# Two re-orderings on VectorE in a hybrid decoder trunk: weight-sum splits before a block's products, and S5 matrix steps spread over two groups

## The reference, cut to what matters

```
h = x + 1/2 * SwiGLU_a(RMSNorm(x))                    # w_ffn1_gu, w_ffn1_down
u = RMSNorm(h); P = u @ W_in                          # GLA heads and S5 heads
h = h + concat(GLA out, S5 out) @ W_out
h = h + CrossAttn(RMSNorm(h), memory K/V)
h = h + 1/2 * SwiGLU_b(RMSNorm(h))                    # w_ffn2_gu, w_ffn2_down
y = RMSNorm_final(h)
swiglu(x) = (silu(g) * u) @ w_down, with g, u = split(x @ w_gu)
S5: ab = exp(dt*L); bb = (ab - 1)/L * b; x_t = ab * x_{t-1} + bb u_t; y = Re(C x) + D u
```

## Time and profile before

| | |
|---|---|
| median of 3 runs | 1297.46 us (1296.92 to 1297.63) |
| the profiled execution | 1296.79 us, of which its span is 1295.0 us |
| TensorE (PE) busy | 1270.0 us, 98% of the span, 10275 matmul records |
| PE weight loads busy | 1230.6 us, 95% |
| VectorE busy | 861.3 us, 67% |
| ScalarE busy | 527.3 us, 41% |
| GpSimd busy | 350.0 us, 27% |

### The profile page before, as it was taken

One profiled execution on the slowest core, in us unless ns is written; L12 is line 12 of the kernel. 1 busy time (PEld: TensorE's weight loads), 2 busy tenths in 40 slices (PEclk: granted clock), 3 DMA queues, 4 the chain that ended last, 5 costly groups with the idle time before them and its releaser, 6 DMA issues.

```text
span 1295.0 us, 24300 instructions
## 1 busy us (share of the span) xinstructions
PE 1270.0 (98%) x10275; PEld 1230.6 (95%) x10275; DVE 861.3 (67%) x1056; ACT 527.3 (41%) x797; POOL 350.0 (27%) x409
## 2 busy tenths in 40 slices
PE   7999999999999999999999999999999999999997
PEld 6999999999999999999999997599999999999997
DVE  4987379844789736558565537478895589637952
ACT  6544145521223422565443224246453255414543
POOL 0025623276896202000002100032230133102321
PEclk9999999999999999999999999999999999999998
DMA  6232233263213442125423656322233323223221
GB/s 185 81 89 82 82 98 98 82 131 88 83 55 85 90 91 63 53 66 153 120 83 97 203 204 225 133 82 79 84 96 85 98 82 99 83 83 96 86 62 73
DMA packets 227148, 129.95 MB, mean 100 GB/s; under 512 B 22240, under 2 KB 221392, under 8 KB 227024
## 3 DMA queue, kind: packets, MB, share of 16 engines
q1 hardware_dynamic: 223168, 123.37, 33.4%
q10 hardware_dynamic: 3872, 5.04, 1.1%
HBM read 121.42 MB, written 5.78 MB: 98 GB/s over the span
## 4 chain that ended last, share of the span: by engine, by line
PE 89%; DVE 6%; ACT 2%; issue 2%; DMA 0%; SPq 0%; DVEq 0%; ACTq 0%
PE PS L723 86%; PE PS L1315 1%; DVE wl L1967 1%; DVE xl L2076 1%; DMA AR<-in_x_prompt 0%; PE PS L791 0%; ACT wh L1453 0%; DVE PS L2055 0%; ACT gua L1599 0%; DVE PS L2221 0%; DVE Hs L2376 0%; PE PS L1401 0%; DVE gua L2151 0%; PE PS L1293 0%; PE PS L933 0%
## 5 line engine op out<-in xcount | busy, mean ns | idle before, releaser
L1453 ACT ACTIVATE wh<-raw 128x1024 fp32r<-128x1024 f32 (+1 forms) x128 | 132.2, 1033 | 377.0 <-PE PS L723 376.9
L723 PE MATMUL PS<-yh,wh 128*128 128x288 f32 x960 | 206.1, 296 | 2.5 <-DVE yl L2164 1.6
L723 PE MATMUL PS<-yl,wh 128*128 128x288 f32 x960 | 205.0, 295 | 0.0
L723 PE MATMUL PS<-yh,wl 128*128 128x288 f32 x960 | 205.0, 295 | 0.0
L1967 DVE TENSOR_TENSOR wl<-raw,wh 128x1024 fp32r<-128x1024 f32 (+1 forms) x128 | 160.1, 1251 | 62.6 <-ACT wh L1453 61.3
L723 PE MATMUL PS<-xh,wh 128*128 128x288 f32 x768 | 171.7, 305 | 0.3 <-DVEq L2146 0.2
L723 PE MATMUL PS<-xh,ARr 128*128 128x288 f32 x768 | 169.5, 296 | 0.3
L723 PE MATMUL PS<-xh,wl 128*128 128x288 f32 x768 | 164.9, 297 | 0.0
L723 PE MATMUL PS<-xl,wh 128*128 128x288 f32 x768 | 164.8, 296 | 0.0
L723 PEld LDWEIGHTS PS<-yh,wh 128*128 128x128 f32 x960 | 154.0, 188 | 4.2 <-DVE yl L2164 1.8
L723 PEld LDWEIGHTS PS<-yh,wl 128*128 128x128 f32 x960 | 154.3, 188 | 0.0
(11 more groups left out here) (370 smaller groups left out, 2217.0 us busy)
## 6 DMA issues: line engine op xcount, KB each, us to landing
raw<-in_w_ffn_gu SPq DMA_DIRECT2D x88, 512.0 KB, 3.9
raw<-in_w_ffn_down SPq DMA_DIRECT2D x32, 512.0 KB, 4.0
raw<-in_w_in SPq DMA_DIRECT2D x16, 512.0 KB, 4.1
raw<-in_w_ckv SPq DMA_DIRECT2D x16, 512.0 KB, 3.9
raw<-in_w_ffn_down SPq DMA_DIRECT2D x16, 384.0 KB, 3.4
Hs<-in_cache_mem_k SPq DMA_DIRECT2D x6, 1024.0 KB, 7.0
raw<-in_w_out SPq DMA_DIRECT2D x8, 512.0 KB, 4.0
raw<-in_w_cq SPq DMA_DIRECT2D x8, 512.0 KB, 5.1
```

The costliest lines, as they stand in the source:

```text
L723: return e.matmul(out, lhsT, rhs, start=start, stop=stop, **kw)
L1453: e.activation(wh[:, n % 2, 0:K * P], raw[:, n % 4, 0:K * P], ACT.Copy).then_inc(w_hi, 1)
```

## The change

Three places of VectorE's code are edited; no instruction is added or taken away, and the streams of all other engines stay as they are.

```diff
             def third_group(i, n, par):
 
                 plain_low(i, n, par, groups[4])
-                matrix_step(3 * i + par)
-                if par:
-                    matrix_step(3 * i + 2)
+                first = 2 * i + par + (max(0, i - 2) if not par else max(0, i - 1))
+                matrix_step(first)
+                if not par and i >= 2:
+                    matrix_step(first + 1)
 
             def third_down(i, n, par):
 
                 normed(groups[5])(i, n, par)
-                if 2 * i + par < 6:
-                    matrix_step(18 + 2 * i + par)
+                matrix_step(16 + 2 * i + par)
...
             for n in range(8):
+                if n == 7:
+                    low_sums(0)
                 e.wait_ge(mm_done, seq(n) + 3)
                 hidden(n // 2, n, n % 2, groups[0])
...
-                elif n == 7:
-                    low_sums(0)
                 plain_low(n // 2, n, n % 2, groups[0])
...
+                if b == 3:
+                    low_sums(FIRST_FFN2)
                 e.wait_ge(mm_done, seq(n) + 3)
                 hidden(i, n, b % 2, g)
                 if b:
                     conv(n + 2)
-                if b == 3:
-                    low_sums(FIRST_FFN2)
                 plain_low(i, n, b % 2, g)
```

## The result

The changed kernel took 1302.31 us (median of 6 runs, 1300.59 to 1304.42) against 1297.55 us of the kernel before on the same chip (6 runs, 1296.87 to 1299.55). The ratio is 1.0037, with an interval of 1.0024 to 1.0049: slower by some 4.8 us. The forecast was 1300.9, in a range of 1297.6 to 1303.0. The profiled execution took 1301.25 us, its span 1299.4 against 1295.0.

A forecast was written before the change was run, and what follows sets the result against it. TensorE, 89% of the last-ending chain, was the bound, so only its waits count. -1.3 - 1.0 + 4.5 - 0.5 + 1.7 = +3.4 us on 1296.79 gave 1300.2; median forecast 1300.9, range 1297.6 to 1303.0.

The forecast's parts named there:

- Edit 1: At two first units, low_sums goes ahead of the block's wait: -0.65 us each, -1.3 us for two.
- The gap before S1: TensorE's stop after product A11 at a first unit, 1.71 us idle, 1.88 us lost; was to go.
- the one before S3: TensorE's wait ahead of product seven at a first unit, to grow from 0.57 to some 1.8 us.
- The rival of full gain: Product seven is ready when TensorE comes, so each first unit gives 1.88 us, 3.76 in all; chance 0.11.
- Edit 2: Group 3's matrix steps: yl unchanged (0), one step behind it instead of two, -1.0 us at the third down block.
- the gap: TensorE's wait at 401.47 before the third down block, 0.84 us idle plus 0.17; was to go whole, -1.0 us.
- one L2219 takes 1.3 to 2.5 us: Single step behind yl, where a pair took 3.8 us; conv was to start by 397.8 and end by 400.1.
- Edit 3: Last two matrix steps: step 23 behind the last down block's work, so TensorE starts the transposes 4.5 us late.
- The refill: In s5_matrices, transpose rounds no longer wait for ScalarE: 7.4 us becomes 6.8 to 6.9, -0.5 us.
- The clock: After the stop before the transposes, clock at 0.50 for some 3.4 us of work: +1.7 us, between 0 and +3.4.

The follow-up runs named there:

- e5: Kernel before with both low_sums ahead of the block's wait, and the last plain block's L2164 put behind the next unit's four sums; 1290.74 us, ratio 0.9955.
- e1: Kernel before with only both low_sums moved ahead of the block's wait; 1295.63 us, ratio 0.9986.
- e3: Changed kernel with the down group's matrix steps given out earlier, none after its last two blocks; 1295.16 us, ratio 0.9992 to the kernel before.
- e4: Changed kernel with 34 unread matmuls ahead of TensorE's wait for the last matrix step; 1302.38 us, ratio 1.0046 to the kernel before.
- e6: Changed kernel with the down group's matrix steps given out earlier, none after its last block; 1296.43 us, ratio 0.9999 to the kernel before.
- e9: Changed kernel with 30 unread matmuls ahead of TensorE's wait for the last matrix step; 1303.44 us, ratio 1.0045 to the kernel before.
- e10: Changed kernel run again without an edit; 1301.57 us, ratio 1.0035 to the kernel before.
- e2: Changed kernel with both low_sums put back, so only the matrix steps are moved; 1303.44 us, ratio 1.0052 to the kernel before.
- e8: e5 with yl ahead of conv as in e7, 15 steps in group 3, nine over down blocks 0 to 6; 1292.27 us, ratio 0.9965.
- e7: Kernel before with group 3's last yl (L2164) ahead of the conv (L1967) that stood in front of it; 1296.20 us, ratio 1.0000.

## Why the prediction came out as it did

**Edit 1: right, a little small.** -0.65 was forecast for each place, -0.91 and -0.93 came. The gap before S1 went and the one before S3 is 1.64 (1.8 forecast). GpSimd's two instructions held up VectorE as worked out; the fourth sum ended only 0.26 us sooner than worked out (80.70 + 1.09 = 81.79 against 82.05), from small overlaps where one instruction follows another. The rival of full gain is excluded in the changed kernel. e5 shows that the place of the sums, behind the low part and in GpSimd's way, stood against it: with the sums moved ahead each place gives 2.9 us by the ratio, 3.2 to 3.3 in the trace.

The rule that the prediction took from the Trainium skill ("SBUF — State Buffer", section "Who interferes with whom"), that a VectorE instruction with two inputs in SBUF and a GpSimd instruction that reads SBUF exclude each other, agrees with this trace: 2.27 us for L2062, which takes 0.68 alone (in e1, at 67.52). It does not agree as plainly with the rows beside L655: the step ended 0.53 us before L655, where the sums end some 0.5 us behind GpSimd's instruction, and in the trace before the `conv` of 399.07, with two inputs in SBUF, ran from start to end while L655 is shown running (395.96 to 402.33). So those rows don't tell who waited for whom.

**Edit 2, the step with a wrong size.** I gave 0 for `yl` and -1.0 for the gap. `yl` came 0.38 later, within the range given: against TensorE's own work L2148 started 0.41 later, behind the moved steps, L2151 took 0.26 less and L2164 0.22 more. Where the clock stayed (e3, e4, e6) the gap kept 0.40 us idle: it gave 0.44. The step that failed is "one L2219 takes 1.3 to 2.5 us", from which the gap was to go whole: it took 4.79, since I had looked only for how long L2219 took in other places, and not for which GpSimd instruction comes next. The trace before had it in the same stretch, 6.37 us long from 395.96.

The trace of e9 shows that this meeting is not fixed by the code. Its code is that of the change up to `s5_matrices`, and VectorE and TensorE ran:

```profile
394.74 2.43 DVE L2221 TENSOR_TENSOR AR<-AR 128x1152 f32<-128x1152 f32 x1
397.76 3.73 DVE L1969 TENSOR_TENSOR wl<-raw,wh 128x768 fp32r<-128x768 f32 x1
```

The step took 2.43 us, as forecast, but then the `conv` was the one beside L655 and took 3.73; the gap kept 0.82 us, and the wait for `yl` was 0.97. So edit 2 gave 0.6 us there, at `yl`, and nothing in e3, e4 and e6. What sets which of the two comes about stays open; e9 started later than the others.

**Edit 3: right.** +4.5 forecast, +4.85 came: L2221 was held up (2.60 us), which I had put at 0.1 to 0.3. TensorE waited 4.7 us for L2223 (4.4 forecast). The refill was 0.63 (0.5 forecast): 6.76 us where there were 7.39, in e4, e6 and e9.

**The clock: right at the stop, missed at `yl`.** +1.7 was forecast behind the stop; 1.89 came in the trace of the change, 1.6 in e10 and 2.3 in e2. The trace agrees with what the Trainium skill says ("TensorE: Matmul & The Clock Gate", section "What's actually happening"), that an idle array drops to 1.2 GHz and comes back only after sustained work. But I let the clock fall at that stop alone. It fell behind the wait for `yl` too, 2.0 us long, in three of six traces with such a wait (the change, e2, e10; not e3, e4, e6), for some 1.5 us. I had argued that it stays through gaps of 1.7 to 1.9 us; a few tenths more are enough in some executions.

**The sum.** Forecast +3.4 on the trace; by the terms measured, -1.84 + 0.38 + 1.5 - 0.99 + 4.85 - 0.63 + 1.89 = +5.2, and by the medians +4.8 and +5.0 (e10). The terms are 1.8 us over the forecast: edit 2 with the second slow stretch, which hides the gap, is 1.9 over (+0.9 for -1.0), edit 3 0.35 and the clock 0.2, while edit 1 and the refill gave 0.7 more than forecast. So part of the miss at `yl` was made up by the small forecast for edit 1, which is luck. The median lies 1.4 us above the forecast, inside the range given for the measurement and at the edge of the forecast's own (1302.3).

That the falls come in some executions and not in others may be one reason for the spread: 3.8 us among the 6 runs of the change, against 2.7 for the kernel before. With e10 alone it is 2.6 and 4.4, so the spread itself shows nothing.

## What to carry to other kernels

Work that is put off towards a barrier costs from the moment when the engine's own last block stands ahead of it: look where the last piece stands in the queue, not how much work there is per block. Before a move, look at which long GpSimd instruction the moved VectorE instruction will meet; the trace before shows which one is near, though not which instruction will meet it in each execution (e9). Putting off an instruction that nobody waits for (e5) brought another 4.0 us, where the move itself had brought 1.8 (by the ratios). And a stop of TensorE of about 2 us or more cost up to 2.3 us here on top of its own length.

## What the runs showed of the hardware

- The clock behind stops of TensorE, from 12 us on and before the end, in the twelve traces: none of 1.0 to 1.8 us was followed by a fall; those of 1.95 to 2.02 us were in three traces of six; those of 2.09 (e9), 2.13 (e8), 2.43 (e4) and 4.7 us (three traces) all were. The fall began inside the stop in two of the three of 4.7 us, and else 0.3 to 1.3 us behind its end. Four traces (before, e1, e3, e5) also have a fall at 1279 to 1284 us, with no idle time of TensorE in the ten microseconds ahead of it; what sets that one off is open.
- A VectorE product of two SBUF operands took 4.79 us beside GpSimd's L655, in the change, e2, e3, e4, e6 and e10, and 2.43 in e9; the other seven of L2219 in the change took 1.3 to 2.6 us.
- The same eight DMA issues took ScalarE 3.7, 4.76 or 5.10 us, by the kernel. Nothing that was tried explains it.
- Matmuls of 288 columns stood 0.130 us apart from 990 to 1034 us in the traces of before and e1, and 0.133 in the ten others. That is 1.2 us in these blocks. The same two spacings show elsewhere: 0.130 in e4 alone from 124 to 166 us, and in e7 alone in the down group of group 3. So a span can differ by such an amount without a cause in the code; what chooses the spacing is open.
